# Three of four prompt token tiles computed with the tokens stationary; the fourth from gathered rows of u

## The reference, cut to what matters

```python
def chunk(xc):
    C = xc.shape[0]
    qh = (xc @ w_q).reshape(C, PEER_HEADS, 2, PEER_KEY_DIM).astype(f32)
    sc = jnp.einsum('chpd,hpnd->chpn', qh, keys.astype(f32))
    ...                      # top 16 of the sums of two scores: indices eidx, weights gate
    ue = u[eidx].astype(f32)
    act = jax.nn.gelu(jnp.einsum('cd,chkd->chk', xc.astype(f32), ue), approximate=False)
    ve = v[eidx].astype(f32)
    return jnp.einsum('chk,chkd->cd', gate * act, ve).astype(x.dtype)
```

## Time and profile before

| | |
|---|---|
| median of three runs | 3343.57 us |
| span of the profiled execution | 3348.3 us |
| granted TensorE clock, mean | 0.987 |
| TensorE busy | 3207.5 us (96%) |
| VectorE busy | 1965.7 us (59%) |
| GpSimd busy | 1854.5 us (55%) |
| ScalarE busy | 1026.8 us (31%) |
| DMA | 988.38 MB, mean 295 GB/s |

### The profile page before, as it was taken

The page is one execution under the profiler, slowest core; times in us unless marked ns, Lnnn a source line. Parts: engine busy times, 40 slices in busy tenths (PEclk is TensorE's granted clock), DMA queues, the critical chain, the costliest instruction groups (busy, mean ns, idle before and its releaser), DMA issues.

```text
span 3348.3 us, 40492 instructions
## 1 busy us (share of the span) xinstructions
PE 3207.5 (96%) x14740; PEld 2633.0 (79%) x14740; DVE 1965.7 (59%) x3363; ACT 1026.8 (31%) x1427; POOL 1854.5 (55%) x1430
## 2 busy tenths in 40 slices
PE   7999899999999999999999999999997999999998
PEld 6677787888888888578878888888886887887886
DVE  3521315995100001855658997888885677887788
ACT  2432222333322222400102333444443232332222
POOL 3034334655544443675564332767677688888871
PEclk9999899999999999999999999999998999999999
DMA  6268677777777777598789998999999999999995
GB/s 233 103 208 274 229 240 295 241 244 240 245 241 240 243 241 270 157 372 313 285 304 363 311 327 293 370 398 393 393 393 408 354 341 321 346 360 342 348 349 179
DMA packets 322538, 988.38 MB, mean 295 GB/s; under 512 B 46896, under 2 KB 80176, under 8 KB 310960
## 3 DMA queue, kind: packets, MB, share of 16 engines
q1 hardware_dynamic: 226960, 708.80, 60.4%
q0 software_dynamic: 91264, 272.96, 22.6%
q10 hardware_dynamic: 4128, 4.19, 0.4%
HBM read 737.28 MB, written 248.51 MB: 294 GB/s over the span
## 4 chain that ended last, share of the span: by engine, by line
PE 60%; issue 16%; POOL 15%; DVE 5%; DMA 2%; DVEq 1%; another core or an unknown queue 0%; ACT 0%; SPq 0%; POOLq 0%; ACTq 0%
PE ps L1299 18%; PE ps L1301 18%; PE ps L1300 18%; POOL v_row L866 5%; POOL value L849 5%; POOL w_lo L815 4%; PE ps L1604 3%; DVE acc L956 1%; DMA pair<-pair_dram 1%; DMA v_row<-in_v_rows,row_i 1%; DMA pair_dram<-w_lo 0%; PE ps L1522 0%; DMA act_in<-act_dram 0%; DMA lo_dram<-u_lo 0%
## 5 line engine op out<-in xcount | busy, mean ns | idle before, releaser
L1299 PE MATMUL ps<-xt_hi,w_hi 128*128 128x512 f32 (+1 forms) x2424 | 989.1, 408 | 33.4 <-issue 20.9
L866 POOL DMA_INDIRECT v_row<-in_v_rows,row_i x512 | 669.4, 1307 | 518.9 <-DVE acc L956 392.5
L1300 PE MATMUL ps<-xt_lo,w_hi 128*128 128x512 f32 (+1 forms) x2424 | 940.6, 388 | 0.0
L956 DVE SCALAR_TENSOR_TENSOR acc<-v_row,share,acc 128x1024 f32<-128x1024 f32 x512 | 658.0, 1285 | 283.4 <-DMA v_row<-in_v_rows,row_i 225.2
L1301 PE MATMUL ps<-xt_hi,u_lo 128*128 128x512 f32 x2048 | 801.6, 391 | 0.0
L849 POOL DMA_INDIRECT value<-act_dram,value_i x512 | 637.5, 1245 | 202.5 <-issue 153.6
L815 POOL TENSOR_TENSOR u_lo<-u_raw,w_hi 128x512 fp32r<-128x512 f32 x256 | 362.0, 1436 | 345.3 <-ACT w_hi L698 336.9
L1299 PEld LDWEIGHTS ps<-xt_hi,w_hi 128*128 128x128 f32 x2424 | 460.2, 190 | 112.5 <-issue 26.9
L1300 PEld LDWEIGHTS ps<-xt_lo,w_hi 128*128 128x128 f32 x2424 | 460.3, 190 | 71.2 <-issue 0.2
L717 ACT ACTIVATE act_t<-ps 128x512 f32<-128x512 f32 x256 | 153.1, 598 | 968.7 <-PE ps L1301 870.7
L1301 PEld LDWEIGHTS ps<-xt_hi,u_lo 128*128 128x128 f32 x2048 | 385.3, 188 | 82.4
(11 more groups left out here) (220 smaller groups left out, 4117.1 us busy)
## 6 DMA issues: line engine op xcount, KB each, us to landing
u_raw<-in_u_t SPq DMA_DIRECT2D x256, 512.0 KB
pair<-pair_dram SPq DMA_DIRECT2D x69, 1024.0 KB
lo_dram<-u_lo SPq DMA_DIRECT2D x128, 512.0 KB, 5.3
act_dram<-act_t SPq DMA_DIRECT2D x256, 256.0 KB
u_lo<-lo_dram SPq DMA_DIRECT2D x128, 512.0 KB
u_raw<-in_v_rows SPq DMA_DIRECT2D x128, 512.0 KB
w_raw<-in_weights SPq DMA_DIRECT2D x69, 512.0 KB, 5.1
pair_dram<-w_hi SPq DMA_DIRECT2D x69, 512.0 KB, 5.6
```

What stands on the lines that cost most here:

```text
L866: pool.indirect_dma_start(out=v_row[:, i % ROWS_DEEP, :], out_offset=None, in_=v_rows, in_offset=bass.IndirectOffsetOnAxis(ap=row_i[:, tt, ...
L956: dve.scalar_tensor_tensor(out=there, in0=v_row[:, i % ROWS_DEEP, :], scalar=share[:, tt, k:k + 1], in1=there, op0=ALU.mult, op1=ALU.add). ...
L1299: pe.matmul(where, lh, rh, start=first, stop=False)
L1300: pe.matmul(where, lh, rl, start=False, stop=False)
```

## The change

- Prompt, pass 1: the tokens become the stationary operand and u the moving one. A tile is now a quarter of four expert tiles: two of the eight chunks of the inner dimension for 512 experts (`load_u`: 512 pieces of 1 KB instead of 128 of 4 KB). TensorE does 2 x 3 x 3 = 18 matmuls of 128 x 512 for a tile, for token tiles 1, 2 and 3 only (`DENSE`). Gelu runs on three banks behind every fourth tile. The three results are stored by SP one group later (`store_prompt_acts`), in the same program order behind `store_rows`.
- VectorE turns each tile of u in 32 x 32 squares (`turn_u`, four transposes of 128 x 256), spread over `choose` by a count of nanoseconds (`beside`, `TURN_PACE`), and the rest behind it. Behind each group of four tiles SP stores the turned tile to `u_rows` with eight DMAs of 32 partitions, 256 KB each in pieces of 1 KB (`store_rows`). The stores to `lo_dram` go. SP waits for `u_turned` before it loads u tile n+4. `u_lo` has two buffers, not four.
- Token tile 0 of the prompt: its 128 products are made in the sample's layer. GpSimd gathers rows of `u_rows`, VectorE multiplies and sums (`take_dot`), ScalarE applies gelu to 128 x 128 numbers. These 128 dots and the 512 rows of v are one list of 640 items. 34 items stand before the first attention scores, 5 in each of the 8 units (before: 3 rows), 7 before each merge up to 128 (before: 6), 8 behind the merges, 2 for each query tile, 8 and 4 in the last part. 384 values are gathered, not 512.
- Sample, pass 1: the reloads from `lo_dram` go. GpSimd makes the small part for tiles 0 to 48 and asks for two values beside each; VectorE makes it from tile 49 on (`rest_of_u`). `choose` takes no rows. The gates start at tile 47. `spread_batch` becomes one operation on 128 x 1024 and eight TENSOR_SCALARs on 128 x 128. Beside the gates stand 2.5 items a tile, behind them 3.
- Pass 2 has the remaining 249 items over 122 tiles (before: 204 rows, each with a value while there are any).
- Smaller: the first token tile of the prompt is stored to `x_dram` in pieces of 128 bytes; the scaling of the prompt's residual waits for it.

```diff
+EXPS_AT = [18, 44, 71, 94]
+
+
+CHOICE_AT = [12, 23, 34, 45]
+GATES_AT = 47
 SPLIT_P_AT = 9
...
+FETCHED = 1
+DENSE = list(range(FETCHED, NT))
+QUARTERS = 4
+SQUARE = 32
+WIDE = QUARTERS * P
+PROMPT_ACTS = EXPERT_TILES // QUARTERS * len(DENSE)
+DOTS = FETCHED * HK
+VALUES = len(DENSE) * HK
 GATHERS = NT * HK
...
+TURN_PACE = 2400
+
+
+FQK_ITEMS, UNIT_ITEMS, MERGE_ITEMS, OUT_ITEMS, QUERY_ITEMS, PLE_ITEMS = 34, 5, 7, 8, 2, (8, 4)
+VALUES_FROM = FQK_ITEMS + UNITS * UNIT_ITEMS
+VALUES_BESIDE = 2
+
...
-        u_lo_at = [42, 46, 62, 58]
-        u_lo = [at(f"u_lo{k}", kb, [P, D], F32R) for k, kb in enumerate(u_lo_at)]
+        u_lo = [[at(f"u_lo{s}{k}", kb, [P, D], F32R) for k, kb in enumerate(where)] for s, where in enumerate(((62, 58), (42, 46)))]
...
+        x_row = acc[:, 1, :]
+        stage = [[at(f"stage{k}{h}", kb, [P, 2, P // SQUARE, D // 4]) for h, kb in enumerate(where)] for k, where in enumerate(((82, 42), (66, 74)))]
...
+                group, quarter = divmod(n, QUARTERS)
+                chunks = slice(2 * P * quarter, 2 * P * (quarter + 1))
+                sp.dma_start(u_raw[:, n % DEEP, :].rearrange("p (j c) -> p j c", j=QUARTERS),
+                             u_t[group * QUARTERS:(group + 1) * QUARTERS, :, chunks].rearrange("j p c -> p j c")).then_inc(u_in[n % DEEP], 16)
...
+            def store_rows(group):
+
+                for half in range(2):
+                    first = (group * QUARTERS + 2 * half) * P
+                    for q in range(P // SQUARE):
+                        there = u_rows[first:first + 2 * P, q * D // 4:(q + 1) * D // 4].rearrange("(g i) c -> i g c", i=SQUARE)
+                        here = stage[group % 2][half][q * SQUARE:(q + 1) * SQUARE].rearrange("i j b c -> i (j b) c")
+                        sp.dma_start(there, here).then_inc(rows_stored[group % 2], 16)
...
+            def store_prompt_acts(group):
+                for d in range(len(DENSE)):
+                    a = group * len(DENSE) + d
+                    sp.wait_ge(act_made, 2 + a + 1)
+                    sp.dma_start(prompt_act[d, :, group * WIDE:(group + 1) * WIDE], act_t[:, a % DEEP, :]).then_inc(act_stored[a % DEEP], 16)
...
+                        sp.wait_ge(u_turned, n + 1)
                         if n + DEEP < EXPERT_TILES:
-                            load_u(n + DEEP)
-                        if reloaded(n):
-                            sp.dma_start(lo_dram[n], u_lo[n % DEEP][:].bitcast(F32)).then_inc(u_lo_stored[n % DEEP], 16)
-                        store_act(s, n)
+                            load_u(s, n + DEEP)
+                        if n % QUARTERS == QUARTERS - 1:
+                            store_rows(n // QUARTERS)
...
+                        if n % QUARTERS == QUARTERS - 1:
+                            group = n // QUARTERS
+                            for d in range(len(DENSE)):
+                                gelu(group * len(DENSE) + d, n, len(DENSE) * (group % 2) + d)
...
-                def gelu(n):
+                def gelu(n, tile, bank):
                     slot = n % DEEP
-                    act.wait_ge(w_used, made(mu + n))
-                    act.wait_ge(act_stored[slot], deep_landed(e0 + n, slot))
-                    act.activation(act_t[:, slot, :], ps[:, n % 2, :], ACT.Gelu).then_inc(act_made, 1)
+                    act.wait_ge(w_used, made(mu + tile))
+                    act.wait_ge(act_stored[slot], deep_landed(a0 + n, slot))
+                    act.activation(act_t[:, slot, :], ps[:, bank, :], ACT.Gelu).then_inc(act_made, 1)
...
+            def fetch_items(upto):
+
+                while asked < upto:
+                    if asked < DOTS:
+                        fetch_item(u_rows, *divmod(asked, HK))
+                    else:
+                        tt, k = divmod(asked - DOTS, HK)
+                        if tt == 0 and k == 0:
+                            pool.wait_ge(row_taken, DOTS)
+                            fetch_acc(1)
+                        if tt and k == 24:
+                            store_prompt(tt - 1)
+                        if tt >= 1 and k == 40 and tt + 1 < NT:
+                            pool.wait_ge(prompt_stored[tt - 1], 16)
+                            fetch_acc(tt + 1)
+                        fetch_item(v_rows, tt, k)
+                    if asked > VALUES_FROM:
+                        fetch_value()
+
...
+            pool.wait_ge(x_stored, 16 * FETCHED * P // SQUARE)
+            pool.wait_ge(resid_stored, 16 * NT)
+            pool.wait_ge(row_i_made, NT)
+            for k in range(2):
+                pool.wait_ge(rows_stored[k], 128 * (EXPERT_TILES // QUARTERS // 2))
+            pool.dma_start(x_row, x_dram[0]).then_inc(x_back, 16)
+            fetch_acc(0)
+            fetch_items(VALUES_FROM)
+            for slot in range(DEEP):
+                pool.wait_ge(act_stored[slot], 16 + 16 // DEEP * PROMPT_ACTS)
+            fetch_items(ITEMS_LAYER)
+            for n in range(BY_POOL):
+                pool.wait_ge(w_hi_made, STREAM + n + 1)
+                split(u_lo[1][n % 2][:], w_hi[:, (STREAM + LAYER_TILES + n) % 2, :], u_raw[:, n % DEEP, :])
+                for _ in range(VALUES_BESIDE):
                     fetch_value()
-                    rows_asked += 1
-
-            for slot in range(DEEP):
...
+            def take_dot(i):
+
+                k, there = i % HK, v_row[:, i % ROWS_DEEP, :]
+                if k == 0:
+                    dve.wait_ge(x_back, 16)
+                dve.wait_ge(row_in[i % ROWS_DEEP], 16 * (i // ROWS_DEEP + 1))
+                dve.scalar_tensor_tensor(out=there, in0=there, scalar=1.0, in1=x_row, op0=ALU.mult, op1=ALU.mult,
+                                         accum_out=value[:, 0, k:k + 1]).then_inc(row_taken, 1)
+                if k == HK - 1:
+                    dve.drain().then_inc(dots_made, 1)
...
+            def turn_u():
+
+                nonlocal turned
+                n, slot = turned, turned % DEEP
+                group, quarter = divmod(n, QUARTERS)
+                if n == 0:
+                    dve.wait_ge(w_lo_made[1], made(LAYER_TILES - 1))
+                if n == QUARTERS:
+                    dve.wait_ge(resid_stored, 16 * NT)
+                if quarter == 0 and group >= 2:
+                    dve.wait_ge(rows_stored[group % 2], 128 * (group // 2))
+                dve.wait_ge(u_in[slot], deep_landed(n, slot))
+                for half in range(2):
+                    for k in range(2):
+                        at_k = (2 * quarter + k) * SQUARE
+                        d = dve.transpose(stage[group % 2][half][:, :, :, at_k:at_k + SQUARE].rearrange("p j b i -> p (j b) i"),
+                                          u_raw[:, slot, :].rearrange("p (j k b i) -> p j k b i", j=QUARTERS, k=2, i=SQUARE)[:, 2 * half:2 * half + 2, k])
+                d.then_inc(u_turned, 1)
+                turned += 1
+
...
+            def beside(s, ns):
+
+                nonlocal spent
+                if s:
+                    return
+                spent += ns
+                while spent >= TURN_PACE and turned < EXPERT_TILES:
+                    spent -= TURN_PACE
+                    turn_u()
+
...
+                for i in range(BATCH):
+                    d = dve.tensor_scalar(hot_row[:, j, i, :], iota[:], all_t[:, 0, t0 + i:t0 + i + 1], all_t[:, 2, t0 + i:t0 + i + 1],
+                                          ALU.is_equal, ALU.mult)
+                d.then_inc(hot_made, 1)
...
+            def rest_of_u(n):
+                dve.wait_ge(w_hi_made, STREAM + n + 1)
+                dve.tensor_tensor(u_lo[1][n % 2][:], u_raw[:, n % DEEP, :], w_hi[:, (STREAM + LAYER_TILES + n) % 2, :].bitcast(F32),
+                                  ALU.subtract).then_inc(u_lo_made, 1)
...
-                        m, lo = mu + n, u_lo[n % DEEP][:]
-                        pe.wait_ge(act_made, n + 1)
-                        for k in range(KD):
-                            if k % (KD // 2) == 0:
-                                pe.wait_ge(w_lo_made[k // (KD // 2)], made(m))
-                            w = slice(k * P, (k + 1) * P)
-                            mm = three(ps[:, n % 2, :], w_hi[:, m % 2, w], lo[:, w], xt_hi[:, k, :], xt_lo[:, k, :], k == 0, k == KD - 1)
+                        m, lo = mu + n, u_lo[0][n % 2][:]
+                        group, quarter = divmod(n, QUARTERS)
+                        if quarter == 0 and group >= 2:
+                            pe.wait_ge(act_made, 2 + len(DENSE) * (group - 1))
+                        for half in range(2):
+                            pe.wait_ge(w_lo_made[half], made(m))
+                            k, here = 2 * quarter + half, slice(half * WIDE, (half + 1) * WIDE)
+                            for d, tt in enumerate(DENSE):
+                                mm = three(ps[:, len(DENSE) * (group % 2) + d, :], xt_hi[:, k, cols_of(tt)], xt_lo[:, k, cols_of(tt)],
```

(1 more changed line is left out.)

391 lines of the change are left out of this document (199 added, 192 removed).

## The result

The changed kernel takes 3723.01 us (3720.65 to 3726.49, 4 runs) against 3343.57 us: 1.1134 times the kernel before, 95% interval [1.1117, 1.1151], slower by 11%. A fourth run of the kernel before took 10869.4 us, three times the others, and is left out of the comparison. Forecast were 3407 us. The sign was the likelier one, the size lies far outside the range.

The account below looks back on a forecast made before the run. TensorE, busy 96% of the span, was taken as the bound. Span 3348.3 - 3 (pass 1) + 10 + 12 + 7 + 15 + 12 + 10 = 3411, less 4.7 to the median: 3407 us; range 3235 to 3530, slower at 0.65.

Parts of the forecast that it names:

- The ring of pass 1: Prompt's pass 1: gelus wait for activation stores behind row stores; 21.7 us a group against 16.3 us of matmuls.
- TensorE's granted clock ... I charge nothing: Pass 1: a 5.4 us wait is shorter than the earlier 21 us; no clock loss charged, at most 12% of 699 us.
- Tile 4g+5 itself: 4.08 us: Link of pass 1's ring: TensorE's 18 matmuls of this tile, before ScalarE may copy tile 4g+7; 4.08 us.
- The last link: Pass 1: from SP's row stores to the group's last gelu; 10.9 us, between 9.2 and 14.6.
- VectorE in pass 1: 512 transposes at 0.41 us, 210 us; VectorE sums to 478 us and is the bound only above 0.82 us a transpose.
- (a): Start of the sample's layer: GpSimd starts late, 34 items before the first scores at 2.4 us each; 10 us (0 to 20).
- (b): Sample's attention: two more items in each of 8 units on VectorE; 12 us, at least 7, at most 21.
- (c): Sample's merges: from item 74 each item has a value, 17.2 us of GpSimd against 16.3 of TensorE; 7 us (0 to 15).
- (d): Sample's pass 1 to tile 48: GpSimd's split halves and two values, 5.8 against 5.44 us a tile; 15 us (0 to 25).
- (e): Sample's gates: VectorE's work 7.6 against 7.33 us a tile; 12 us, 0 to 120, by the port rule 100 us.
- (f): Pass 2: rows rise from 1.67 to 2.04 a tile, VectorE 5.2 of 5.44 us; 10 us (-5 to 40).
- The rival of slow stores: Pass 1: row stores from 32 partitions are slower than other packets, ring 25.4 us, 111 us more, 3518 us; chance 0.25.

Follow-up runs that it names:

- a2: Changed kernel with each group's row stores as two DMAs from 128 partitions in place of eight from 32; 3648.0 us, ratio 1.0902 to the kernel before.
- b1: a1 with 20 in place of 34 items before the sample's first scores, 9 in place of 7 a merge; 3465.2 us, ratio 1.0350.
- b2: a1 with 3 in place of 5 items in each attention unit, 9 in place of 7 a merge; 3473.2 us, ratio 1.0397.
- c3: b4 with three row buffers in place of four throughout; 3681.2 us, ratio 1.0982 to the kernel before.
- b3: a1 without values fetched beside the splits of the sample's first 49 tiles, fetched later with rows; 3496.0 us, ratio 1.0452.
- b4: a1 with two rows in place of 2.5 beside each gate batch, two for three behind; 49 rows moved to pass 2; 3453.1 us, ratio 1.0327.
- d1: c1 without the two values beside each of the sample's first 49 splits; 3420.5 us, ratio 1.0232 to the kernel before.
- b6: a1 with the gates' one-hot rows made by two operations on 1024 columns in place of eight on 128; 3482.2 us, ratio 1.0399.
- a3: Changed kernel with both a1's order and a2's two row stores from 128 partitions; 3425.9 us, ratio 1.0245 to the kernel before.
- d2: c1 with GpSimd making the small part of u for every second tile beside the gates; 3429.7 us, ratio 1.0247.
- a1: Changed kernel with SP issuing the activation stores ahead of the eight row stores; 3457.7 us, ratio 1.0335 to the kernel before.
- c2: c1 plus b4's edit: six row buffers and two rows a gate batch, 49 more rows in pass 2; 3387.9 us, ratio 1.0126.
- c1: a1 with six row buffers in place of four from the end of the sample's layer on; 3379.6 us, ratio 1.0094.

## Why the prediction was wrong, step by step

- **The ring of pass 1**: the mechanism and two links right. Landed store to TensorE 3.0 us (third gelu 1262.83, TensorE 1265.77: 2.9); copy and split 3.7 us (1272.69 to 1276.42). Two were mis-sized. **The step that failed is "TensorE's granted clock ... I charge nothing"** together with "Tile 4g+5 itself: 4.08 us". It took 6.9 us, since the clock fell in the pause. The pause was 7.4 to 10.8 us and not the 5.4 us that I worked out, but that is no excuse: behind a2's pauses of 5.3 to 6.6 us the clock had fallen too. The reason that I gave, that 5.4 us are shorter than the 21 us of the earlier trace rows, was none; no row of before had a pause of that length. 2.8 us in each of 30 groups are 84 us, and TensorE's busy time says 78 (568 against 490 us). The prediction's own upper bound, 12% of 699 us, is 84.
- **The last link**: 10.9 us forecast (9.2 to 14.6), 13.3 in the group shown (1276.42 to 1289.70). 2.4 x 30 = 72 us. With what is left, 18 us that I haven't traced, pass 1 and the start of the layer are +171 us, where I had -3. That SP's stores land in order, as the prediction says, doesn't show: it has the issues alone. The changed kernel shows it, in the mean of groups 3 to 29: the last row store landed 11.6 us behind the first one's issue, the three of activations at 12.2, 12.9 and 13.5.
- **VectorE in pass 1**: 512 transposes at 0.412 us (forecast 0.41), and it isn't the bound. That the figure is right to the digit is luck, as it came from another operation with as many columns.
- **(a), (b)** start and attention: 22 us forecast, 50 measured (68.7 + 141.7 against 70.7 + 89.4). TensorE stood 25.7 us at the first scores, because VectorE was still taking the 34 items (b1); two more a unit cost as much (b2). I had priced the items by VectorE's 1.285 us and a start of 10 us; the run of them goes at about 2 us each. That the buffers set this price is what c3 speaks for. The 2.4 us for a row beside the pairs were also summed wrong: by the prediction's own numbers it is 1.32 x 5.44 / 2.80 = 2.6 us, and 34 rows are 87 us, not 82.
- **(c)** merges 7, measured 12.
- **(d)** 15, measured 26: 277.3 us for 47 tiles is 5.90 a tile. Values are 14 of it (b3).
- **(e)** gates 12, measured 79, inside its bounds. I summed VectorE's work to 7.6 us a tile against a tile of 7.33. The work was 481 / 64 = 7.5 us, right; what failed is that a sum of work was taken for the pace. The wait for rows, 225 us in the whole kernel before, was left as it was, though the change asked for more rows a tile through the same four buffers.
- **Behind the gates**, +30 us: no term in the prediction (17 tiles with three items each).
- **(f)** pass 2 10, measured 4. The near hit is luck in part: at b4's 2.3 us the 45 rows more would cost about 100 us, and at d1's 0.5 us the 182 values that pass 2 fetched before and no longer does would give back about as much (an estimate from these runs). The prediction priced neither so.

Measured less forecast: pass 1 174, (a) and (b) 28, (c) 5, (d) 11, (e) 67, behind the gates 30, (f) -6: 309 of the 311 us between the two spans. Of the 174 the clock and the last link make 156. The rival of slow stores (3518 us) was real in part: it put the last link 3.7 us over the forecast, measured were 2.4, and a2, whose stores are faster, still takes 3648 us. That the port costs what the rule in (e) gives is refuted by b6 (530 us or less if it did, 571 measured).

Open stays how far more buffers would make an item cheaper in the attention and beside the merges: there memory is full, and only fewer were tried (c3). Open are also what the six issues fewer do in a2 and a3, and why d2 got slower.

## What to carry to other kernels

Where a wait closes a ring, price it twice: once for itself, once for the clock that TensorE loses in the pause, and look first for an order of issues that opens it; here two swapped calls were worth 265 us. Where a queue of n buffers feeds an engine, ask how long one buffer takes to come back (taken, issue, landing) against how long n of them last at the new rate, before summing the engine's work. And work moved from a full engine to three half-full ones is free only where none of these stands in such a ring. With the stores first, pass 1 is 113 us shorter than before (589 against 702), and the stages of the sample are 222 us longer; with six buffers these are still 130 us longer.

## What the runs showed of the hardware

- Row stores from 32 partitions: the same 2.1 MB in 1 KB packets from 128 partitions, in two DMAs and not eight, shortened the last link from 13.0 to 10.9 us, and with a1's order took 1 us a group off; a packet took 47 in place of 54 ns. By the Trainium skill (SBUF — State Buffer, Door 1: The DMA port swizzle) 32 partitions reach half of the ports; the runs agree in direction, and by its rate I had put 3 us.
- An issue on SP is not of one length: 0.37 us for a load at 1276.42, 7.54 us for the eight 256 KB stores behind it, 0.94 each. Thinned to 32 KB each, eight took 3.9 us.
- A row's price depended on the buffers in flight: 2.3 us in pass 2 with four (b4 against a1), 1.5 us with six (c2 against c1), with VectorE's operation at 1.285 us.
- TensorE's granted clock was 0.50 to 0.63 over the first 12 matmuls behind pauses of 5.3 to 6.6 us (a2), and these matmuls started up to 0.44 us apart in place of 0.23.
